# Layer norms between TensorE's tiles: partial sums inside the last tile, another order of the norm's operations, and the first two weight units interleaved by chunk

## The reference

```python
h = layer_norm(x, ln_in_g, ln_in_b)
for l in range(DEPTH_2):                      # 2 layers
    proj = h @ w_in[l]
    ...                                       # four mixers: conv, attention, gated unit, latent attention
    mix = jnp.concatenate([o_a, o_b, o_c, o_d], axis=-1) @ w_out[l]
    h = layer_norm(DEEPNORM_ALPHA * h + mix, ln_mix_g[l], ln_mix_b[l])
    up = depthwise_conv(h @ ffn_w_up[l], ffn_conv_w[l], ffn_conv_b[l])
    f = (jax.nn.silu(up[..., :D_FF]) * up[..., D_FF:]) @ ffn_w_down[l]
    h = layer_norm(DEEPNORM_ALPHA * h + f, ln_ffn_g[l], ln_ffn_b[l])

def layer_norm(x, g, b):
    mu = jnp.mean(x, axis=-1, keepdims=True)
    xc = x - mu
    var = jnp.mean(xc * xc, axis=-1, keepdims=True)
    return xc * lax.rsqrt(var + LN_EPS) * g + b
```

## Time and profile before

| | |
|---|---|
| median of three runs | 2146.91 us (2146.41 to 2148.29) |
| the profiled execution | 2146.85 us, of which the span of its trace is 2145.0 us |
| TensorE busy | 96% of the span, mean granted clock 0.991 |
| VectorE, ScalarE, GpSimd busy | 55%, 37%, 8% |
| start of the four norms (first L1320) | 1164.27, 1533.40, 1758.20, 2127.34 us |

### The profile page before, as it was taken

The page is one execution under the profiler, slowest core; times in us unless marked ns, Lnnn a source line. Parts: engine busy times, 40 slices in busy tenths (PEclk is TensorE's granted clock), DMA queues, the critical chain, the costliest instruction groups (busy, mean ns, idle before and its releaser), DMA issues.

```text
span 2145.0 us, 24832 instructions
## 1 busy us (share of the span) xinstructions
PE 2063.4 (96%) x10090; PEld 1441.7 (67%) x10090; DVE 1186.6 (55%) x1800; ACT 786.0 (37%) x1199; POOL 164.3 (8%) x118
## 2 busy tenths in 40 slices
PE   6999999999999999899999999999999999999997
PEld 4797788843333333357567888888785678888885
DVE  6556534323333323357876764656677757646565
ACT  4546534321212211254673422222445734222233
POOL 1000000010000000000100120102001001101020
PEclk9999999999999999999999999999999999999998
DMA  5342242489999999922102222233131022222321
GB/s 200 114 148 78 79 177 89 181 350 426 426 427 427 427 426 427 402 81 98 54 2 79 98 98 99 84 113 116 62 118 54 2 79 98 98 98 84 109 93 49
DMA packets 40913, 357.61 MB, mean 167 GB/s; under 512 B 6096, under 2 KB 7288, under 8 KB 13152
## 3 DMA queue, kind: packets, MB, share of 16 engines
q1 hardware_dynamic: 36448, 342.99, 41.1%
q0 software_dynamic: 4064, 10.95, 1.6%
q10 hardware_dynamic: 288, 2.10, 0.2%
HBM read 354.94 MB, written 6.83 MB: 169 GB/s over the span
## 4 chain that ended last, share of the span: by engine, by line
PE 84%; DMA 6%; DVE 4%; ACT 3%; issue 2%; SPq 0%; DVEq 0%; ACTq 0%
PE bank L1130 41%; PE bank L2120 10%; PE bank L482 9%; DMA H<-in_expert_up_w 5%; PE bank L497 4%; PE bank L504 3%; PE bank L1912 2%; PE bank L1897 1%; PE bank L1928 1%; PE bank L2145 1%; PE bank L1157 1%; PE bank L2213 1%; ACT S L1977 1%; ACT S L1988 1%; PE bank L476 1%
## 5 line engine op out<-in xcount | busy, mean ns | idle before, releaser
L1130 PE MATMUL bank<-split_x_high,split_weights 128*128 128x512 f32 x1888 | 586.3, 390 | 0.1
L1130 PEld LDWEIGHTS bank<-split_x_high,split_weights 128*128 128x128 f32 x1888 | 354.5, 188 | 76.5 <-issue 3.3
L1391 ACT ACTIVATE split_weights<-ring 128x2048 fp32r<-128x2048 f32 (+1 forms) x113 | 211.1, 1868 | 531.2 <-PE bank L1130 468.0
L1383 DVE TENSOR_TENSOR split_weights<-ring,split_weights 128x2048 fp32r<-128x2048 f32 (+2 forms) x115 | 258.5, 2248 | 164.2 <-ACT split_weights L1391 164.1
L1130 PE MATMUL bank<-split_products,split_weights 128*128 128x512 f32 x1136 | 302.7, 389 | 0.0
L1130 PE MATMUL bank<-split_x_low,split_weights 128*128 128x512 f32 x736 | 286.3, 389 | 0.0
L1130 PEld LDWEIGHTS bank<-split_products,split_weights 128*128 128x128 f32 x1136 | 213.3, 188 | 44.5 <-issue 0.5
L2120 PE MATMUL bank<-split_x_high,split_weights 128*128 128x512 f32 x480 | 152.5, 396 | 6.3 <-DVE split_x_low L2322 6.3
L1130 PEld LDWEIGHTS bank<-split_x_low,split_weights 128*128 128x128 f32 x736 | 138.2, 188 | 28.6
L1107 POOL TENSOR_TENSOR QKVG<-QKVG 128x512 f32<-128x512 f32 x44 | 97.9, 2226 | 551.8 <-DVE QKVG L1594 466.3
L711 DVE SCALAR_TENSOR_TENSOR S<-S,stats,bank 64x512 f32<-64x512 f32 x32 | 23.7, 740 | 180.2 <-ACT S L837 180.1
(11 more groups left out here) (474 smaller groups left out, 3203.0 us busy)
## 6 DMA issues: line engine op xcount, KB each, us to landing
ring<-in_ffn_w_up SPq DMA_DIRECT2D x44, 1024.0 KB, 4.8
ring<-in_w_in SPq DMA_DIRECT2D x24, 1024.0 KB, 4.8
QKVG<-in_expert_gate_w SPq DMA_DIRECT2D x11, 2048.0 KB, 20.5
AUX<-in_expert_up_w SPq DMA_DIRECT2D x11, 2048.0 KB, 25.2
QKVG<-in_expert_down_w SPq DMA_DIRECT2D x11, 2048.0 KB, 25.9
MKV<-in_expert_gate_w SPq DMA_DIRECT2D x11, 2048.0 KB, 24.1
ring<-in_expert_up_w SPq DMA_DIRECT2D x11, 2048.0 KB, 29.5
ring<-in_expert_down_w SPq DMA_DIRECT2D x11, 2048.0 KB, 23.2
```

What stands on the lines that cost most here:

```text
L1130: mm = pe.matmul(acc[:, :], w[:, u, k, m], x, start=first and q == 0, stop=last and q == 2)
L1383: st.tell(dve.tensor_tensor(w[:, 1, 0:ks, 0:nc_], raw_half(g)[:, :, 0:nc_], as_f32(w[:, 0, 0:ks, 0:nc_]), ALU.subtract), wl_done)
L1391: st.tell(act.activation(WHL[g % 2][:, 0, 0:ks, 0:nc_], raw_half(g)[:, :, 0:nc_], ACT.Copy), wh_done)
```

## The change

The two matmuls with sum_x and sum_sq go from `layernorm` into `partial_sums`, called ahead of the last two chunks of the last tile. The square of the mean is made straight from PSUM and ahead of minus the mean; VectorE makes the variance ahead of all its centrings, and GpSimd waits for the variance as well. ScalarE makes the halves of the second unit's high weights before Ln and behind Exp. `first_pair` takes both units behind a norm together: each chunk is multiplied with the first unit's high and low weights and the second's high ones; the second's low parts follow at the end. It is used behind norms 0, 1 and 2. In the first layer's input units `high_first` and `low_last` stay.

```diff
@@ GpSimd
             def centred_by_gpsimd(use):
-                pool.wait_ge(ln_mean, 2 * use + 1)
+                pool.wait_ge(ln_mean, 2 * use + 2)
+                pool.wait_ge(ln_vard, use + 1)
                 for c in range(LN_SPLIT, DC):
                     st.tell(pool.tensor_tensor(X[:, c, :], X[:, c, :], sum_x[:, :], ALU.add), ln_pool)
@@ TensorE
+                def first_pair(g, accs, before, low, done):
+
+                    w, w2 = WHL[g % 2], WHL[(g + 1) % 2]
+                    cut = [slice(i * P, (i + 1) * P) for i in range(2)]
+
+                    def lows(k):
+                        pe.wait_ge(xl_done, before + k + 1)
+                        for i in range(2):
+                            mm = pe.matmul(accs[i][:, :], w[:, 0, k, cut[i]], low[:, k, :], start=False, stop=k == DC - 1)
+                            if k == DC - 1:
+                                mm.then_inc(done, 1)
+
+                    pe.wait_ge(wl_done, g + 1)
+                    for k in range(DC):
+                        pe.wait_ge(xh_done, before + k + 1)
+                        for i in range(2):
+                            for u in range(2):
+                                pe.matmul(accs[i][:, :], w[:, u, k, cut[i]], XH[:, k, :], start=k == 0 and u == 0, stop=False)
+                        if k == 0:
+                            pe.wait_ge(wh_done, g + 2)
+                        for i in range(2):
+                            pe.matmul(accs[2 + i][:, :], w2[:, 0, k, cut[i]], XH[:, k, :], start=k == 0, stop=False)
+                        if k:
+                            lows(k - 1)
+                    lows(DC - 1)
+                    for i in range(2):
+                        for k in range(DC):
+                            pe.matmul(accs[2 + i][:, :], w2[:, 0, k, cut[i]], low[:, k, :], start=False, stop=False)
+                    pe.wait_ge(wl_done, g + 2)
+                    for i in range(2):
+                        for k in range(DC):
+                            mm = pe.matmul(accs[2 + i][:, :], w2[:, 1, k, cut[i]], XH[:, k, :], start=False, stop=k == DC - 1)
+                        mm.then_inc(done, 1)
...
+                def partial_sums(use, a, b):
+                    pe.wait_ge(x_summed, use + 1)
+                    pe.matmul(bank[a][:, :], ones, sum_x[:, :], start=True, stop=False)
+                    pe.wait_ge(sq_added, (DC - 2) * (use + 1))
+                    pe.matmul(bank[b][:, :], ones, sum_sq, start=True, stop=False)
...
+                            if m == N_OUT - 1 and i == 1 and k == order[-3]:
+                                partial_sums(2 * l, 7, 5)
...
                 def layernorm(use, a, b, last_add, idle):
-                    pe.wait_ge(x_summed, use + 1)
-                    pe.matmul(bank[a][:, :], ones, sum_x[:, :], start=True, stop=False)
                     pe.wait_ge(r_free, last_add)
                     pe.matmul(bank[a][:, :], ones, X[:, DC - 1, :], start=False, stop=True).then_inc(ln_stat, 1)
-                    pe.wait_ge(sq_added, (DC - 2) * (use + 1))
-                    pe.matmul(bank[b][:, :], ones, sum_sq, start=True, stop=False)
                     pe.wait_ge(ln_squared, DC * (use + 1))
...
                 layernorm(2 * l, 7, 5, l * NR_DONE + DC, 4)
+                first_pair(UA + l * NU + NF, bank[0:4], (2 * l + 1) * DC, XL, f_done)
...
+                                if n == len(ffn) - 1 and i == 1 and k == ks - 3:
+                                    pe.wait_ge(r_free, (l + 1) * NR_DONE - 2)
+                                    partial_sums(2 * l + 1, 4, 5)
@@ VectorE
                 centred = {}
                 dve.wait_ge(ln_mean, 2 * use + 1)
-                for c in range(1):
-                    centred[c] = centre(c)
-                dve.wait_ge(ln_mean, 2 * use + 2)
                 dve.wait_ge(ln_stat, 2 * use + 2)
                 step(dve.scalar_tensor_tensor(rstd[:, :], bank[b][:, :], 1.0 / D, rstd[:, :], ALU.mult, ALU.subtract))
                 st.tell(dve.tensor_scalar(rstd[:, :], rstd[:, :], 0.0, None, ALU.max), ln_vard)
-                for c in range(len(centred), 3):
+                dve.wait_ge(ln_mean, 2 * use + 2)
+                for c in range(3):
                     centred[c] = centre(c)
@@ ScalarE
                 act.wait_ge(ln_stat, 2 * use + 1)
+                st.tell(act.activation(rstd[:, :], bank[a][:, :], ACT.Square, scale=1.0 / D), ln_mean)
                 st.tell(act.activation(sum_x[:, :], bank[a][:, :], ACT.Identity, scale=-1.0 / D), ln_mean)
-                st.wait()
-                st.tell(act.activation(rstd[:, :], sum_x[:, :], ACT.Square), ln_mean)
+                if split:
+                    w, raw, half = WHL[unit % 2], raw_half(unit), DC // 2
+                    act.wait_ge(half_landed[unit % 2], 16 * (unit // 2 + 1))
+                    act.wait_ge(*unit_used(unit - 2))
+                    st.do(act.activation(w[:, 0, 0:half, :], raw[:, 0:half, :], ACT.Copy))
                 act.wait_ge(ln_vard, use + 1)
...
                 st.tell(act.activation(rstd[:, :], rstd[:, :], ACT.Exp, scale=-0.5), ln_rstd)
+                if split:
+                    st.tell(act.activation(w[:, 0, half:DC, :], raw[:, half:DC, :], ACT.Copy), wh_done)
...
```

More of the change, by code:

```diff
@@ L1177, in in_unit @@
                             mm.then_inc(t_done, 1)
-                for a in range(5):
+                if l:
+                    first_pair(UA + l * NU, [free_tile(name) for a in range(2) for name in IN_UNITS[a]], 2 * l * DC, XI, t_done)
+                for a in range(2 if l else 0, 5):
                     in_unit(a)
@@ L1355, in layer_tensor @@
                     done = f_done if kind == "up" else r_done
-                    if n == 0:
-                        high_first(banks, w, (2 * l + 1) * DC, XL, done)
-                    elif n == 1:
+                    if kind == "down" and b == 0:
+                        for k in range(ks):
+                            pe.wait_ge(pl_done, l * FC + PARTS[a][0] + k + 1)
+                            for i in range(2):
+                                mm = products(i, k, k == 0, k == ks - 1)
+                                if k == ks - 1:
+                                    mm.then_inc(done, 1)
+                    else:
                         for i in range(2):
-                            low_last(banks[i], w, slice(i * P, (i + 1) * P), g, lambda k: XH[:, k, :], lambda k: XL[:, k, :]).then_inc(done, 1)
-                    else:
-                        if kind == "down" and b == 0:
                             for k in range(ks):
[L1364 to L1369, removed]
-                            for i in range(2):
-                                for k in range(ks):
-                                    mm = products(i, k, k == 0, k == ks - 1)
-                                mm.then_inc(done, 1)
+                                mm = products(i, k, k == 0, k == ks - 1)
+                                if n == len(ffn) - 1 and i == 1 and k == ks - 3:
+                                    pe.wait_ge(r_free, (l + 1) * NR_DONE - 2)
+                                    partial_sums(2 * l + 1, 4, 5)
+                            mm.then_inc(done, 1)
                 pe.wait_ge(f_free, (l + 1) * 2 * FC)
-                pe.wait_ge(r_free, (l + 1) * NR_DONE - 2)
                 layernorm(2 * l + 1, 4, 5, (l + 1) * NR_DONE, 4 if l + 1 < L2 else 0)
@@ L1649, in bias @@
                     st.tell(act.activation(X[:, c, :], X[:, c, :], ACT.Identity, bias=b(c)), ln_ready)
-                if split:
-                    w, raw, half = WHL[unit % 2], raw_half(unit), DC // 2
-                    act.wait_ge(half_landed[unit % 2], 16 * (unit // 2 + 1))
-                    act.wait_ge(*unit_used(unit - 2))
                 for c in range(DC):
@@ L1658, in normed @@
                         act_x_high(act, st, b, c)
-                        if c == 1:
-                            st.do(act.activation(w[:, 0, 0:half, :], raw[:, 0:half, :], ACT.Copy))
-                        if c == 3:
-                            st.tell(act.activation(w[:, 0, half:DC, :], raw[:, half:DC, :], ACT.Copy), wh_done)
                         if c >= 4:
```

5 lines of the change are left out of this document (3 added, 2 removed).

## The result

| | before | after |
|---|---|---|
| median, 13 runs each | 2146.99 us (2144.88 to 2149.58) | 2152.61 us (2150.70 to 2154.15) |
| ratio, 95% interval | | 1.0023 (1.0016 to 1.0030) |
| profiled execution, span | 2146.85, 2145.0 | 2153.65, 2151.8 |

The account below looks back on a forecast made before the run. TensorE, busy 96% of 2145.0 us, was taken as the bound. Norms 0 to 2 add 3 x 0.53 = 1.6, norm 3 adds 2.5: +4.1 on 2146.85, median 0.06 above, so 2151.0 us, range 2146.4 to 2155.5.

Parts of the forecast that it names:

- Norm 3: The last norm, with no products behind it: its stream of scalings was to end 2.5 us later.
- Insertion: Two statistics matmuls moved ahead of the last tile's last six products: 0.97 us lost, as cover under the last addition goes.
- Variance first: Centring no longer precedes the variance: no gain; three centrings instead of two put the first scaling at T+7.76 instead of T+7.01.
- L1437 at 0.46: VectorE's not-below-zero operation on the variance, with GpSimd held until its end, takes 0.46 us instead of 0.95.
- The rival of 0.95: Not-below-zero operation stays at 0.95 us, GpSimd not having slowed it: +0.49 in four norms, 2153.0; chance 0.08.
- Collision: VectorE's first two scalings meet GpSimd's later centrings, running T+7.76 to T+10.94; VectorE's stream of chunks is 2.22 us late.
- The rival without a collision: First scaling keeps 0.75 us beside GpSimd; three norms gain 1.8, the last loses 0.75: 2145.9; chance 0.17.
- the full rule: Port lock held for a whole GpSimd operation: second scaling waits 0.28 us more in each of four norms, 2152.1.
- Interleaving: Both units behind a norm taken together: TensorE restarts T+10.24, ends T+32.38 against T+31.85, costing 0.53 us a norm.
- The third unit's low half: VectorE's weight work for the third unit, 6.86 us within 7.3: about 0.4 of cover left.
- Clock: Rival: TensorE's pause before the first product, 2.05 against 1.53, halves its clock; 1.3 us a norm, 2154.9; chance 0.20.
- the border: Measurement tells 0.2%, 4.3 us, from no change: slower begins at 2151.2; chances slower 0.46, same 0.52, faster 0.02.

Follow-up runs that it names:

- changed_again: The changed kernel itself, unaltered, measured again beside the kernel with six filler matmuls: 2151.25 us, ratio 1.0018.
- pair_alone: Kernel before plus the interleaved pair of units and ScalarE's half copies of the second unit's high weights: 2142.99 us, ratio 0.9977.
- stats_back: Changed kernel with both partial-sum matmuls put back behind the last tile: 2149.89 us, one run.
- stats_in_alone: Kernel before with only the two partial-sum matmuls moved inside the last tile: 2154.26 us, one run.
- no_pair: Changed kernel without the interleaving, first unit by chunk and second as a whole: 2156.56 us, one run.
- gpsimd_one_column: Changed kernel with GpSimd's three centrings cut to one column of 512: 2146.69 us, one run.
- Six fillers: Changed kernel with six instead of four filler matmuls behind the statistics: 2151.61 us, ratio 1.0017; repeated, 2150.71 us, ratio 1.0019.
- gpsimd_early: Changed kernel with GpSimd waiting for minus the mean alone, not for the variance: 2149.20 us, one run.
- pair_clamp_psum: As pair_alone, with the variance written to PSUM and the not-below-zero operation reading it there: 2143.01 us, ratio 0.9978.

## Why the prediction was right

The mechanism and its sum held; the median lies above the sum by an amount that stays open. Where no fall lies in the stretch, after against before is +0.58 and +0.50 at norms 1 and 2, and +0.53, +0.60 and +0.50 at norms 0 to 2 in the profile of changed_again; 0.53 was forecast. Norm 3 gave +2.44 in both; 2.5 was forecast. That profile's span is 2149.3, 4.3 above before's, with 4.1 forecast.

The experiments price the parts, each added to the one above it (us at norm 1, where no fall lies in these runs; us at norm 3):

| part | how measured | norm 1 | norm 3 |
|---|---|---|---|
| interleaving | pair_alone less before | -1.31 | -0.01 |
| order of the norm, GpSimd later | stats_back less pair_alone | +0.92 | +1.49 |
| insertion | after less stats_back | +0.97 | +0.96 |
| sum | | +0.58 | +2.44 |

These prices hold in this order only. Going through the runs the other way (before, stats_in_alone, no_pair, changed kernel; no_pair has ScalarE's copies of the second unit where the change has them), the insertion costs 1.7 to 1.8 at norms 0 and 2 and 1.79 at norm 3, the new order only 0.1 to 0.2 and 0.64 more, and the interleaving gives back 1.4 and nothing. The sum is the same. With the old order the inserted sums bring a collision of their own (L1443 in stats_in_alone), so insertion and order can't be priced apart.

Step by step:

- **Insertion.** At norm 0 the last product ends at T+1.74 (1167.36 and the 0.23 of a product; forecast 1.83), the mean matmul starts at T+2.69 (2.77), the variance at T+4.78 (4.86). Right to 0.09. At norms 1 and 3 the mean matmul starts at T+2.78, and the insertion costs 0.97 and 0.96; at norm 2 it costs 0.88 (32.36 against stats_back's undisturbed 31.48).
- **Variance first.** I wrote that taking the centring from in front of the variance gains nothing. That holds with the sums where they were; stats_in_alone shows that it does not hold behind the insertion, where the order before would have lost another 0.28, and 0.50 in the collision with GpSimd. This didn't touch the sum, since the changed kernel has the new order.
- **L1437 at 0.46.** Measured 0.43, with GpSimd behind it. The rival of 0.95 is out.
- **Collision.** Two scalings 3.16; forecast 3.18 (T+7.76 to T+10.94). gpsimd_one_column shows the cause. The rival without a collision is out. The first scaling pays 0.75 (1.49 against 0.74), the second 1.01, the price of the earlier trace rows; in all 52 cases in the traces of this case a caught scaling ends 0.55 behind the GpSimd operation that it met, and so does L1527 in the earlier trace rows (1649.05, against 1648.50 for the first of the three GpSimd operations). The Trainium skill (SBUF — State Buffer, "SBUF: two separate sides") has an exclusive lock, held for the whole instruction. The traces agree: the price depends on how much of the GpSimd operation is left. The prediction took the 1.02 as less than a whole operation of 1.30, and 2152.1 as what the full rule would give. That was a wrong reading. A GpSimd operation that meets nothing takes 1.27, and a scaling caught at its very start would end 0.55 behind it: 1.82 instead of 0.74, so by this estimate a caught scaling pays 1.08 at most. (The prediction also ends GpSimd's third centring near T+9.9, where its own 6.15 and 3.90 make 10.05; nothing hangs on it.)
- **Interleaving.** Restart T+10.03 (10.24), pause 1.92 (2.05), chunk 1 at T+11.62 (11.93), chunk 3 at T+15.47 (15.60), done at T+32.36 (32.38). The step from a scaling's end to its products, 0.99 in the forecast, was 0.90 for chunk 0 and 0.81 for chunk 1. Two small misses cancel in the 32.36, so that its agreement to 0.02 is luck: chunk 3 came 0.13 early, since the second scaling ended at T+10.81 instead of T+10.94, and its eight products took 1.93 instead of 1.81. TensorE waits for nothing there; the second product starts 0.34 behind the first instead of 0.227, as it does behind every wait (0.30 to 0.34 in the changed kernel's trace, norms 1 and 2). The third unit's low half was in time at every norm. At norm 2 it ended at T+31.95, 0.4 ahead of its first product, the cover that was forecast.
- **Clock.** The rival came in part: one fall in three norms of the profiled execution, 1.1 instead of the 1.3 I gave it (33.52 against 32.38 to 32.45), none in the profile of changed_again. Forecast and rival are thus not two cases but a mixture. Six fillers took the pause away and no measured time with it (0.5 between the medians), so falls behind the norms are not shown to be what lifts the median.

Of the +6.8 of the profiled span, 1.58 lies in the first block. It is no effect of the change: T at norm 0 is 1165.85 here and 1164.43 in changed_again, the same kernel; pair_alone, whose block is the same, has 1165.84, stats_back 1164.67, before 1164.27. The medians differ by 5.6 in the first comparison and by 4.0 in changed_again; the trace's 4.1 without falls fits the second, and whether falls or scatter make the rest of the first is not settled. The prediction set the border between "same" and "slower" at 2151.2 and gave "slower" 0.46; the median of 2152.61 lies beyond it by 1.4, which the mechanism does not explain.

## What to carry to other kernels

A matmul that runs while its engine waits for another is free; moving it ahead of the wait costs its whole length (here both sums went ahead of the wait, 1.74 with the return to the products; only one of them, 0.86, had stood in its cover, and that is what was lost, with 0.1 for the return), so look first for the operation whose time the wait already covers. Before delaying a helper engine, list the operations it will then run beside and where their inputs lie: GpSimd next to VectorE operations with sources in SBUF cost 1.2 a norm, next to operations from PSUM nothing. And change one thing at a time: a gain of 1.3 a norm was hidden here under losses of 1.9, and the two parts that lose can't be priced apart.

## What the runs showed of the hardware

- A VectorE operation caught by a GpSimd one ends a fixed time behind it, so it pays by how much of it is left. The not-below-zero operation ended 0.28 to 0.29 behind GpSimd's record in four kernels: it took 0.43 alone, 0.95 arriving 0.61 into the GpSimd operation (before), 1.07 arriving 0.49 into it (gpsimd_early), 1.44 arriving 0.11 into it (stats_in_alone). Scalings ended 0.55 behind: 1.19 arriving 0.62 into it (gpsimd_early), 1.49 arriving 0.33 into it (after), 0.74 alone.
- Two inputs from SBUF are not needed for that: the not-below-zero operation has one, and writes SBUF. With its source in PSUM it took 0.69 and ended 0.04 behind GpSimd's record, and the third GpSimd operation took 1.28 instead of 1.45 (pair_clamp_psum against pair_alone).
- The collision costs both engines. The third GpSimd operation of a norm in the changed kernel has a record of 1.72 where a free one has 1.27. The 0.45 are its own wait for the first scaling, so that the second scaling, issued 0.52 into this record, has nearly the whole operation ahead of it and pays 1.01.
- A pause of TensorE of 1.92 to 2.4 was followed by a fall to 0.50 for one stretch at some norms (after norm 0; stats_back norms 0 and 2; stats_in_alone and no_pair norm 1) and not at others of the same kernels, nor in gpsimd_early at 2.28. Behind pauses of 1.5 (before, pair_alone) and 0.2 (six fillers) none was seen at a norm.
- A fall costs 1.1 to 1.15 where TensorE is otherwise busy (after, stats_back). Where it waits for chunks inside the first unit it cost less: under 0.05 in no_pair, about 0.3 in stats_in_alone.
